# RWKV core: keys and r in two buffers and staged a pass ahead, solved blocks returned in rows that hold both operands, scratch zeroed during the projections

## The reference, cut to what matters

```python
def mixer_rwkv(...):
    r, k, v = xr @ wr, xk @ wk, xv @ wv                    # projections, 16 heads of 64
    decay = exp(-exp(-softplus(-(w0 + tanh(xw @ w1) @ w2)) - 0.5))   # one for each direction
    a = sigmoid(a0 + (xa @ a1) @ a2);  g = sigmoid(xg @ g1) @ g2
    kk = k * k_k / norm(k * k_k);      k = k * (1 + (a - 1) * k_a)
    # per token, forward and in reverse, S a 64 x 64 state of each head:
    S = S * decay + (S @ -kk) (kk * a)^T + v k^T;  y = S @ r
    out = (groupnorm(y_f + y_b) * lnx_g + lnx_b + sum(r * k * r_k) * v) * g @ wo
```

## Time and profile before

| what | us |
|---|---|
| median of 3 runs | 3223.96 (3219.43 to 3233.72) |
| profiled execution, its own time | 3224.59 |
| its span, first to last instruction | 3222.9 |
| PE busy in the span | 2492.6 (77%) |
| DVE, ACT, POOL busy | 814.1, 479.3, 330.0 |
| mean granted clock of PE | 0.902 of full speed |

### The profile page before, as it was taken

One profiled execution on the slowest core, in us unless ns is written; L12 is line 12 of the kernel. 1 busy time (PEld: TensorE's weight loads), 2 busy tenths in 40 slices (PEclk: granted clock), 3 DMA queues, 4 the chain that ended last, 5 costly groups with the idle time before them and its releaser, 6 DMA issues. The chain is left out here.

```text
span 3222.9 us, 41458 instructions
## 1 busy us (share of the span) xinstructions
PE 2492.6 (77%) x18136; PEld 1218.7 (38%) x18136; DVE 814.1 (25%) x1765; ACT 479.3 (15%) x960; POOL 330.0 (10%) x488
## 2 busy tenths in 40 slices
PE   4489995537396888888885995888887788888887
PEld 0134442324143433333332442777785322222222
DVE  1201404555403111111113303556552210000001
ACT  0100003222102000000002002434331100000001
POOL 0000000034101000000002203243440000000000
PEclk9899997769698999999998996999998888989998
DMA  9632200000024799999994123222221899999996
GB/s 378 282 107 78 78 26 1 0 1 1 8 87 184 290 411 421 420 412 422 407 393 148 55 88 111 54 56 54 56 44 60 332 400 404 405 410 418 405 409 277
DMA packets 208613, 692.39 MB, mean 215 GB/s; under 512 B 122200, under 2 KB 140416, under 8 KB 158896
## 3 DMA queue, kind: packets, MB, share of 16 engines
q1 hardware_dynamic: 207312, 689.25, 54.3%
q10 hardware_dynamic: 1120, 0.48, 0.1%
HBM read 675.82 MB, written 13.84 MB: 214 GB/s over the span
## 5 line engine op out<-in xcount | busy, mean ns | idle before, releaser
L1424 PE MATMUL bank<-moe_w,moe_xT 128*64 128x512 f32 (+3 forms) x3072 | 634.8, 569 | 70.6 <-DMA moe_w<-in_exp_w 68.2
L1448 PE MATMUL bank<-moe_w,moe_hidT 128*64 128x512 f32 (+1 forms) x1408 | 377.8, 692 | 126.1 <-DMA moe_w<-in_exp_w 114.3
L1424 PEld LDWEIGHTS bank<-moe_w,moe_xT 128*64 128x64 f32 (+1 forms) x3072 | 198.2, 126 | 511.7 <-issue 405.2
L1448 PEld LDWEIGHTS bank<-moe_w,moe_hidT 128*64 128x64 f32 (+1 forms) x1408 | 108.6, 139 | 360.5 <-issue 217.5
L1516 DVE TENSOR_TENSOR moe_silu<-bank,moe_silu 64x512 f32<-64x512 f32 (+3 forms) x96 | 56.5, 639 | 668.1 <-ACT moe_silu L1479 668.1
L1529 DVE COPY moe_rows<-bank 32x512 f32<-32x512 f32 x96 | 65.9, 686 | 529.6 <-PE bank L1448 528.7
L1479 ACT ACTIVATE moe_silu<-bank 64x512 f32<-64x512 f32 (+3 forms) x96 | 46.2, 546 | 1031.6 <-PE bank L1424 1031.6
L402 PE MATMUL bank<-w_slab,mixT 128*128 128x512 f32 x384 | 166.2, 593 | 1.9 <-PE bank L402 1.6
L1558 POOL TENSOR_TENSOR moe_xn<-moe_xn,moe_w 128x1024 f32<-128x1024 f32 x6 | 18.1, 3020 | 1432.6 <-ACT moe_w L1495 1432.6
L399 PE MATMUL bank<-mixT,w_slab 128*128 128x512 f32 x320 | 140.8, 601 | 10.5 <-DMA w_slab<-in_ab_w_in 9.4
L1672 PE MATMUL bank<-mixture,rw_slab 128*128 128x512 f32 (+1 forms) x384 | 143.6, 527 | 4.5 <-PE bank L1672 3.7
(11 more groups left out here) (469 smaller groups left out, 3049.5 us busy)
## 6 DMA issues: line engine op xcount, KB each, us to landing
moe_w<-in_exp_w SPq DMA_DIRECT2D x256, 1408.0 KB, 13.9
moe_w<-in_exp_w SPq DMA_DIRECT2D x64, 2048.0 KB, 18.9
ada_slab<-in_ada_w SPq DMA_DIRECT2D x32, 1536.0 KB, 12.8
moe_w<-in_exp_w SPq DMA_DIRECT2D x32, 1536.0 KB, 7.0
w_slab<-in_ab_w_in SPq DMA_DIRECT2D x11, 2048.0 KB, 7.5
wo_slab<-in_ab_w_out SPq DMA_DIRECT2D x16, 512.0 KB, 3.5
x_inv_and_t<-x_blocks SPq DMA_DIRECT2D x64, 128.0 KB, 3.3
rw_slab<-in_rw_wk SPq DMA_DIRECT2D x4, 1024.0 KB, 7.3
```

The costliest lines, as they stand in the source:

```text
L1424: mm = pe.matmul(g.ps[k][64 * m:64 * m + M, 0:hi - lo], xg[:, i % 2, j, c, :], wa[:, sl, m, r, lo:hi], start=(c == 0), stop=(c == DC - 1))
L1448: mm = pe.matmul(g.ps[5 + m][64 * m:64 * m + M, :], hidt[:, c, :], wb[:, sl, c - lo, 512 * m:512 * m + 512], start=(c == 0), stop=(c == FC ...
```

## The change

- `k0` and `r0` get two buffers, chosen by the pass's parity. `stage(i)` now waits for the readers of pass i - 2 (`hats`, `kmod`) and, since the small weights still have one buffer, for `lg` of pass i - 1. `stage(0)` and `stage(1)` are both issued ahead of the passes, and `stage(i + 2)` at the end of pass i's part of SP's queue.
- x_blocks keeps both operands of a row side by side: 128 elements in a row. The four writes go to `at = k * LC` in it, and four reads with rows of 128 take the place of eight with rows of 64. The waits for the reads count 64 where they counted 128.
- x_blocks is zeroed in `stage_rwkv_project`, by six DMAs from `g.ta`, which is all zero until ACT writes its upper half; that ACT copy now waits for the six. The clearing of a tile and the four DMAs before the passes are gone.

```diff
@@ stage_rwkv_project @@
             def _(sp):
                 n = 0
                 for name in "kvr":
                     for q in range(4):
+                        if n == RING:
+                            for d in range(2):
+                                for part in range(3):
+                                    sp.dma_start(g.xscr[d].rearrange("(p f) -> p f", p=P)[:, 344 * part:344 * part + 344], g.ta[:, 0:344]).then_inc(s_zero, 16)
                         if n >= RING:
                             sp.wait_ge(s_free, n - RING + 1)
...
+                sp.wait_ge(s_zero, 96)
...
                 act.wait_ge(s_mm, 2)
+                act.wait_ge(s_zero, 96)
                 act.activation(g.ta[0:64, :], g.ps[1][0:64, :], ACT.Copy).then_inc(s_ev, 1)
@@ stage_rwkv @@
-    PITCH = LC // BL * BL * (LC + 1)
+    NP, XP = LC // BL * BL * LC + LC, LC // BL * (2 * BL * LC + BL)
...
-    def by_row(x, h):
+    def by_row(x, h, pitch, row):
-        return x.rearrange("(c e) -> c e", e=PITCH)[NCH * h:NCH * (h + 1), 0:LC * LC].rearrange("c (b x) -> b c x", x=LC)
+        return x.rearrange("(c e) -> c e", e=pitch)[NCH * h:NCH * (h + 1), 0:LC * row].rearrange("c (b x) -> b c x", x=row)
-    def by_block(x):
+    def by_block(x, row, at):
-        return x.rearrange("(q e) -> q e", e=BL * (LC + 1))[:, 0:BL * LC].rearrange("q (r x) -> q r x", x=LC)[:, :, 0:BL]
+        return x.rearrange("(q e) -> q e", e=BL * (row + 1))[:, 0:BL * row].rearrange("q (r x) -> q r x", x=row)[:, :, at:at + BL]
...
-        k0, r0, v0 = sb("k_pair", [P, T]), sb("r_pair", [P, SEG]), two("v_pair", [P, T])
+        k0, r0, v0 = two("k_pair", [P, T]), two("r_pair", [P, SEG]), two("v_pair", [P, T])
...
-                pool.memset(invs[1][0][:, :, :, :], 0.0).then_inc(S["cleared"], 1)
...
-                sp.wait_ge(S["cleared"], 1)
-                for d in range(2):
-                    for k in range(2):
-                        sp.dma_start(yscr[d, k].rearrange("(p f) -> p f", p=P), invs[1][0][:, :, :, :].rearrange("p c k t -> p (c k t)")[:, 0:2 * NCH * PITCH // P]).then_inc(S["zeros"], 16)
-                sp.wait_ge(S["zeros"], 64)
...
                 def stage(i):
                     if i:
-                        W(sp, "hats", i - 1, 2, 2)
-                        W(sp, "kmod", i - 1, 1, 1)
                         W(sp, "lg", i - 1, 1, 1)
                     if i >= 2:
+                        W(sp, "hats", i - 2, 2, 2)
+                        W(sp, "kmod", i - 2, 1, 1)
                         W(sp, "tokmm", i - 2, 7, 1)
...
                 stage(0)
+                stage(1)
                 for i in range(DC):
...
-                    if i + 1 < DC:
-                        stage(i + 1)
                     W(sp, "nwritten", i, 64, 64)
...
-                            sp.dma_start(by_block(yscr[d, k]), yt[HALF[d], 1 - k if d == 0 else k, :, :]).then_inc(S["xwritten"], 16)
+                            sp.dma_start(by_block(g.xscr[d], 2 * LC, k * LC), yt[HALF[d], 1 - k if d == 0 else k, :, :]).then_inc(S["xwritten"], 16)
                     W(sp, "xwritten", i, 64, 64)
                     for d in range(2):
-                        for k in range(2):
-                            for h in range(2):
-                                sp.dma_start(invs[i % 2][d][HALF[h], :, k, :], by_row(yscr[d, k], h)).then_inc(S["inv"], 16)
+                        for h in range(2):
+                            sp.dma_start(invs[i % 2][d][HALF[h], :, :, :].rearrange("p c k t -> p c (k t)"), by_row(g.xscr[d], h, XP, 2 * LC)).then_inc(S["inv"], 16)
+                    if i + 2 < DC:
+                        stage(i + 2)
@@ DVE and ACT: k0[:, :] becomes k0[i % 2][:, :], r0[:, :] becomes r0[i % 2][:, :] @@
```

More of the change, by code:

```diff
@@ L1766, in stage_rwkv @@
         yc = sb("y_chan", [P, SEG])
-        names = ("starts", "cleared", "zeros", "staged", "col", "kk", "kksq", "kksum", "kkroot", "lw", "sig", "la", "iclr", "lg", "gate", "cum", "bonus_in", "bonus_mm", "kmod", "exps", "hats", "bars", "dg",
+        names = ("starts", "staged", "col", "kk", "kksq", "kksum", "kkroot", "lw", "sig", "la", "iclr", "lg", "gate", "cum", "bonus_in", "bonus_mm", "kmod", "exps", "hats", "bars", "dg",
                  "mm1", "nt", "n1", "nwritten", "nblock", "xblock", "xwritten", "inv", "mask", "nlev", "pmm", "pcopy", "xmm", "xadd", "tokmm", "tok", "nkvmm", "nkv", "aumm", "au", "au_late", "gmm", "gt", "ownmm", "own", "ylmm", "yl",
@@ L1803, in stage @@
                     if i:
-                        W(sp, "hats", i - 1, 2, 2)
-                        W(sp, "kmod", i - 1, 1, 1)
                         W(sp, "lg", i - 1, 1, 1)
                     if i >= 2:
+                        W(sp, "hats", i - 2, 2, 2)
+                        W(sp, "kmod", i - 2, 1, 1)
                         W(sp, "tokmm", i - 2, 7, 1)
-                    for dst, src in ((k0[:, :], g.rwk[:, i, :]), (v0[i % 2][:, :], g.rwv[:, i, :]), (r0[:, :], g.rwr[:, i, :]),
+                    for dst, src in ((k0[i % 2][:, :], g.rwk[:, i, :]), (v0[i % 2][:, :], g.rwv[:, i, :]), (r0[i % 2][:, :], g.rwr[:, i, :]),
                                      (w2s[0:64, 0, :], g.a["rw_w2"][0, 0, :, cols]), (w2s[64:128, 1, :], g.a["rw_w2"][0, 1, :, cols]), (a2s[0:64, :], g.a["rw_a2"][0, :, cols]),
@@ L1897, in keys @@
                     dv.step(dve, dve.tensor_scalar(km[:, :], al[:, :], 1.0, q[:, 4:5], ALU.subtract, ALU.mult))
-                    dv.step(dve, dve.scalar_tensor_tensor(km[:, :], km[:, :], 1.0, k0[:, :], ALU.add, ALU.mult))
-                    dv.step(dve, dve.tensor_tensor(bon[i % 3][:, :], r0[:, :], km[:, SEG:T], ALU.mult))
+                    dv.step(dve, dve.scalar_tensor_tensor(km[:, :], km[:, :], 1.0, k0[i % 2][:, :], ALU.add, ALU.mult))
+                    dv.step(dve, dve.tensor_tensor(bon[i % 3][:, :], r0[i % 2][:, :], km[:, SEG:T], ALU.mult))
                     dve.tensor_scalar(bon[i % 3][:, :], bon[i % 3][:, :], q[:, 5:6], None, ALU.mult).then_inc(S["bonus_in"], 1)
@@ L2074, in scaled @@
                         W(act, "hats", i - 1, 2, 2)
-                    act.activation(kk[:, :], k0[:, :], ACT.Copy, scale=par[i % 3][:, 3:4]).then_inc(S["kk"], 1)
+                    act.activation(kk[:, :], k0[i % 2][:, :], ACT.Copy, scale=par[i % 3][:, 3:4]).then_inc(S["kk"], 1)
                 def roots(i):
@@ L2274, in pmm @@
                         W(pe, "nlev", i, 4, 4)
-                        W(pe, "inv", i, 128, 128)
+                        W(pe, "inv", i, 64, 64)
                     if n >= 4:
@@ L2528, in layer1 @@
             m = lambda name, shape: g.place(rw, name, shape)
+            g.xscr = g.nc.dram_tensor("x_blocks", [2, 2 * NCH * 4 * 2064], F32).ap()
             g.lev, g.i64, g.bones = m("level_masks", [P, 2, 2, LC]), m("eye64", [P, LC]), m("block_ones", [P, P])
```

17 lines of the change are left out of this document (8 added, 9 removed).

## The result

| | before | after |
|---|---|---|
| median of the runs, us | 3226.91 (7 runs, 3219.43 to 3233.72) | 3203.84 (7 runs, 3197.38 to 3211.07) |
| ratio, with its 95% interval | | 0.9928 [0.9912, 0.9944] |
| profiled execution, its own time | 3224.59 | 3203.67 |
| mean granted clock | 0.902 | 0.907 |

The kernel is faster, but by 23 us, not by 53. The time lies 14 us above the range's upper end.

The account below looks back on a forecast made before the run. The RWKV core was taken as bound by a chain of products with holes from ACT's staging wait. Gains of 44.0 (six middle passes), 3.0 (zeroing), 3.7 (pass 0) and 2.0 (pass 7), 52.7 us, gave 3171 us, range 3160 to 3190.

Parts of the forecast that it names:

- the inverse chain: n_t out to memory, back as blocks, solved by GpSimd, out and back as rows for L2282; 36.0 us forecast.
- TensorE's side, 35.6 us: TensorE's own stretch from n_t to L2282 in the middle passes, 43.3 us less 7.7 with inputs staged a pass ahead.
- The solve at 14.4: GpSimd's block solve within the inverse chain, taken as 14.4 us as in pass 4, against 11.9 in pass 7.
- The front of the chain: n_t sent to n_block requested, 6.25 us, and from there to GpSimd's start, 3.43 us.
- First read to L2282: Return of the solved rows from first x_blocks read to TensorE's product; 6.1 us taken, 8.15 if nothing is gained.
- the two side estimates, 5.5 and 7.0 us: Row return by two skill rules: 5.5 us if 512-byte runs reach line rate, 7.0 by the descriptor cycle count.
- Stage two passes ahead on SP: Eight staging issues, about 5 us, placed on SP's queue behind the x_blocks reads; claimed to cost 0.
- L2282 to next n_t: Stretch of each middle pass after the solved rows arrive; claimed unchanged at 13.0 us.
- x_blocks written to first read, 5.8: Writing and landing of solved blocks before the first read; 5.8 us as in pass 4, against 6.4 in pass 7.
- The rival of 64-byte pieces sharing a row: x_blocks writes land much later because both operands share a row, making the kernel slower; 3235 at 8 us more; chance 0.03.
- Zeroing, 3.0: Removing the tile clearing and four writes between projections and core gains 3.0 us, at no cost to the projections.
- the first, a longer inverse chain: Rival: reads keep 8.15 us or the solve slows, chain 38.05, six passes give 31.5, time 3188; chance 0.13.

Follow-up runs that it names:

- Experiment 6: On top of experiment 1, each direction of x_blocks writes and reads got its own semaphores, and TensorE waits for each direction separately; 3170.79 us, ratio to before 0.9817.
- experiment 1: The changed kernel, with SP waiting for a pass's x_blocks reads to land before issuing the staging for the pass after next; 3196.03 us, ratio to before 0.9916.
- experiment 9: On top of experiment 1, each x_blocks read fills 128 partitions with half the columns, 512-byte pieces kept, values wrong; 3190.58 us, ratio to before 0.9885.
- Experiment 3: The changed kernel with three unused 128x512 products ahead of TensorE's wait for the solved blocks; 3199.43 us, ratio to before 0.9920.
- experiment 7: The changed kernel with staging back between n_back writes and n_block reads, one pass ahead, other parts kept; 3226.12 us, ratio to before 0.9985.

## Why the prediction was wrong

- *What bounds the kernel, and that the inverse chain is late next*: right. The wait moved from ACT's L2075 and PE's L2226 to L2280, fed by exactly that chain.
- *TensorE's side, 35.6 us*: right. n_t to L2280 less its wait is 35.1 to 35.6 us in passes 1 to 6. Experiment 6, where TensorE alone decides, has 34.95 to 35.71.
- *The solve at 14.4*: right, 14.3 to 14.6. GpSimd was held up no more than before (14.0 to 14.6), so the solve of 16.9 us, named as the rule against the change, didn't come.
- *The front of the chain*: n_t to n_block 0.7 us better, n_block to POOL 0.8 us worse, its sum right. Why POOL starts up to 5 us after the request in some passes is not settled.
- *First read to L2282, "I take 6.1"*: this step failed, and even its upper bound of 8.15 was passed: 9.03 on the mean. I read the earlier trace rows as 5.0 us of work for the DMA engines and counted on half as many pieces to shorten it. That did little: in pass 7, with nothing else in flight, the return fell from 8.15 to 7.62 us and the fastest 3 us from 201 GB/s to experiment 1's 225. That is a gain of 0.5 us, not 2.0, and neither of the two side estimates, 5.5 and 7.0 us, was reached. By the Trainium skill (DMA: Bandwidth & Descriptors, Specifications) a transfer needs at least 512 bytes for line rate. These reads had 512 and ran at 225 GB/s, and with the same 512 bytes experiment 9 ran at 295: it was mostly the 64 partitions, and not the piece, that held them.
- *"Stage two passes ahead on SP ... Cost 0"*: failed. I looked for who waits for the staging and who is queued behind it, and not for what it does to the transfer ahead. The eight loads are issued from 2.8 us after the first read on, while the reads still run; that makes about 1 us per pass (experiment 1).
- *"L2282 to next n_t is ... 13.0 us, which the change leaves as it is"*: failed by 1.06 us. The rows were there: L2282 took 1.97 us in both passes with a wait and 1.10 in the one without. I put no price on the clock behind a wait, because I forecast a wait of half a us; at 2.9 to 5.4 us it brought the half clock with it in five of six passes. Experiment 3 and pass 6 show it apart from the wait.
- *x_blocks written to first read, 5.8*: 6.34 measured. It is what pass 7 had before (6.39); that row was the better one. The rival of 64-byte pieces sharing a row didn't come: their landing is 3.2 us on the median, against 3.1.

The tile's row after:

```profile
DMA to landing us min/median/max: 2.5/3.2/4.4
```

- *Zeroing, 3.0*: 3.8 measured, and it costs the projections nothing (181.65 us in both). Copy rw_a_in still waits for its product and not for the zeros:

```profile
1775.22 4.64 SPq L1591 DMA_DIRECT2D x_blocks<-rw_a_in  x6
...
1795.42 0.59 ACT L1696 ACTIVATE rw_a_in<-bank 64x512 f32<-64x512 f32 x1 [6.60 <-PE bank L1678]
```

Of the rivals the first, a longer inverse chain, is what came, with a time of 3188 instead of 3204. It lacked both failed zeros: the staging behind the reads and the clock behind the wait. With n_t to L2280 at 39.6 on the mean and 14.06 behind it, the six passes give 16 and the sum is the measured 23. Two sums of the prediction are rounded high, 6 x 7.3 to 44.0 and the six passes at a chain of 36.9 to 39 (38.5); neither matters here. Experiment 6 has the forecast pass, 48.6 us for 49.0: TensorE's side was right, and the chain had to be shortened by some us more than the change did. That its time is also the forecast 3171 is luck: its stretch gained 64.6 us and not 52.7, since passes 0 and 7 fell too, and its profiled execution reached the core 11.6 us later than the one before.

## What to carry to other kernels

When a wait goes, the next-latest chain has to be summed for every piece with the load that it will then carry: the rate that a transfer reaches once its engines are full, and what is newly queued behind it on the same DMA engines. A chain forecast to be late by about nothing is a risk of both prices at once, the wait and the slower clock behind it. What helped most here was not a better transfer but a finer wait, so that half of the data is asked for, and used, as soon as it is there.

## What the runs showed of the hardware that I had not expected

- Reads of 1 MB into 64 partitions ran at 201 and 205 GB/s with 256-byte pieces, at 225 with 512 bytes and at 255 with 4 KB; into 128 partitions with 512-byte pieces at 295 (each in its fastest 3 us of pass 7).
- Two queues with 64 partitions each got no more together than one: 215 GB/s.
- Eight loads issued behind four reads on the same queue while those ran delayed the product that needs them by about 1 us (9.0 against 8.0).
- The half clock does not follow from a wait's length alone. In experiment 3 waits up to 1.9 us left the stretch at 13.0 us and waits of 2.5 us did not, but in the changed kernel pass 6 kept the full clock after 3.02 us, and in experiment 7 the clock fell to 0.50 in pass 0 after 1.90 us (the row below):

```profile
2028.64 1.15 PE L2279 MATMUL bank<-x_inv_and_t,n_levels 64*64 64x64 f32 x32 [1.90 <-DMA x_inv_and_t<-x_blocks]
```

- The first product to the next n_t can be as long at full clock. In pass 1 of experiment 9 it took 14.29 us with the clock at 1.00 throughout, and TensorE stood 1.13 us inside it for nothing that the trace shows (the first row below). Experiment 6, at full clock and with no wait for the blocks, has 13.4 to 14.0 us in its passes 2 to 5, with such holes of 0.76 and 0.53 us in passes 3 and 4 (pass 3's in the second row). What this is stays open. In passes 1 to 5 of the changed kernel TensorE is busy throughout the slow windows, so there the clock accounts for the 1.1 us.

```profile
2078.96 0.21 PE L2296 MATMUL bank<-p_prod,x_inv_and_t 64*64 64x64 f32 x1 [1.13 <-issue]
```

```profile
2182.04 0.27 PE L2287 MATMUL bank<-x_inv_and_t,n_levels 64*64 64x64 f32 x1 [0.76 <-issue]
```
